# A diffusion trunk step on one core: attention units regrouped so that values, turn and scores of three successive units stand side by side in the weight stream

## The chip, the cores and the metric

The kernel runs on one core of a Trainium2 chip. Its time is device microseconds of one execution; the time before is the median of three runs, 2137.43 us. The engines are named as in the profile: PE is the matrix engine (TensorE), PEld its weight loads, DVE the vector engine, ACT the scalar engine, POOL GpSimd, SP the engine that issues the weight transfers.

## What is computed

Two groups of tokens, 128 context tokens and 256 latent tokens, go through two layers with the same weights (384 token columns in all). A layer is a feed-forward block, a mixing block and a second feed-forward block, each behind a modulated norm. The change is in the mixing block:

```
proj = h @ w_in                                   # 22 blocks of 128 columns, then the gates
a_o = neighbourhood_attention(...)                # NA
b_o = window_attention(rope(q), rope(k), ...)     # SWA, with a sink per head
d_o = softmax(q1 k1) - lam * softmax(q2 k2)       # DF, then @ v, then rmsnorm per head
c_o = hyena(hy_in, lp)                            # long convolution through a DFT
merged = sum_i sigmoid(gate_i) * (branch_i @ w_branch[i])
x = x + g2 * (merged @ w_out)
```

Context tokens attend to context alone; latent tokens also read a cache of 128 keys and values.

## The kernel before

**Tiles.** All weights pass as tiles of 128 output columns through a ring of four buffers: SP loads `raw`, ACT copies it to `hi` (L557, the high part of the split), DVE writes `lo = raw - hi` (L781). For the wider tiles of the gates (1280 columns) DVE makes the first 640 columns of `lo` and POOL the rest (L1197). PE multiplies each of eight 128-row chunks three times (hi by hi, hi by lo, lo by hi), so a tile is 24 matmuls of 384 columns (L1287) into one of four PSUM banks; a gate tile has 6 more for its branch product, into `ps_br`. The split of a tile (the step "feed") is made three tiles before PE needs it.

**The mix.** A layer's mixing block has 22 projection tiles, 32 gate tiles ("fused", four branches of 8, in the order NA, SWA, DF, hyena) and 8 output tiles. Each tile is cut into four parts of 6 matmuls; the fourth part of a gate tile also has the 6 branch matmuls, 12 in all. Between the parts stand the small steps of attention and of the convolution. `mix_plan` writes this order out as one list, and all engines walk that same list, each taking its own share of each step, strictly in order. So the place of a step in the list sets its place in every engine's queue. `paced` spreads a list of steps over a list of parts: a number between two steps is a share of the parts.

**An attention unit.** Each branch has 12 units: block, head half, and token block b = 0, 1, 2. For b = 0 (context) there are 128 keys, else 512 - 128 = 384. A unit has four steps:

- `scores`: PE writes q k into `ps_s` (L1496; the single buffer must be free of the exp before); DVE adds a bias or mask where there is one and takes the negated row maximum (L1062; in SWA also the sink, L1067); ACT takes exp and the row sum into `pr` (L709). DF has two such steps per unit, m = 0 and 1.
- `probs`: DVE alone; it divides by the row sum (L1078, L1088; SWA first L1077), in DF it combines both softmaxes (L1078, L1082 to L1085).
- `turn`: PE transposes `pr` into `ps_t` (L1505, 3 blocks of 128, or 1 for b = 0), ACT copies it to `prT` (L717; the single buffer must be free of the values before).
- `values`: PE multiplies `prT` by the values into `ps_o` (L1522, 6 records in the profile, or 2).

Other small steps that the text speaks of: `short` (DVE alone, a convolution of width 3: L1110 and four times L1114, six per layer, in DF's first half), `gate` (ACT tanh L654, then DVE L986), `rope` (PE L1478, DVE L1044 to L1046, each waiting for the one before), `subnorm`, `subinv`, `subout` (the norm of DF's output), `outs`.

**What orders a feed.** `staged` holds the feed of a tile back until a step of a certain kind comes: `turn` before the change, and at the latest the second part of a projection tile or the fourth of any tile. A `gate` step comes after the first part of the next tile.

Of the kernel before, what the change touches and what calls it, by code (L numbers as in the profile page):

```python
# [35 lines left out]
TB = T // P  # L36
# [22 lines left out]
NA, SWA, DF = range(3)  # L59
# [105 lines left out]
def parts(tiles):  # L165

    return [(*t, part) for t in tiles for part in range(PARTS)]


def paced(tiles, side):  # L170

    out = []
    scale = len(tiles) / sum(x for x in side if not isinstance(x, tuple))
    at, done = 0.0, 0
    for x in side:
        if isinstance(x, tuple):
            out.append(x)
            continue
        at += x * scale
        upto = min(len(tiles), int(at + 0.5))  # L180
        out += tiles[done:upto]
        done = upto
    return out + tiles[done:]


def attention_steps(kind):

    out = []
    if kind == DF:
        out += [("scores", kind, 0, 0), 1.3, ("scores", kind, 0, 1), ("probs", kind, 0), 1.5]
        for u in range(12):
            if u + 1 < 12:
                out.append(("scores", kind, u + 1, 0))
            if u < 6:
                out.append(("short", u))

            if 7 <= u < 7 + TB:  # L200
                out.append(("subinv", 0, u - 7))
            if u == 7 + TB:
                out.append(("subout", 0))
            out += [0.9, ("turn", kind, u), 0.9, ("values", kind, u), 0.1]
            if u + 1 < 12:
                out += [("scores", kind, u + 1, 1), ("probs", kind, u + 1)]
            out.append(1.5)
            if u % 6 == 5:
                out += [("square", u // 6), 0.6, ("subnorm", u // 6)]
        return out + [0.8] + [("subinv", 1, b) for b in range(TB)] + [0.6, ("subout", 1), 0.2]  # L210
    out += [("scores", kind, 0, 0), ("probs", kind, 0), 1.5]
    for u in range(12):
        if u + 1 < 12:
            out.append(("scores", kind, u + 1, 0))
        out += [1.0, ("turn", kind, u)]
        if u + 1 < 12:
            out.append(("probs", kind, u + 1))
        out += [1.2, ("values", kind, u), 0.2]
        if u % 6 == 5:
            out.append(("outs", kind, u // 6))  # L220
    return out


def staged(plan):

    out, fed, gates = [], [], []

    def flush(what):
        out.extend(what)
        what.clear()

    for s in plan:
        tile = s[0] in ("proj", "fused", "out")
        if tile and s[-1] == PARTS - 1:
            flush(fed)
        out.append(s)
        if tile and s[-1] == 0:  # L240
            fed.append(("feed", *s))
            flush(gates)
        if s[0] == "turn" or s[0] in ("proj", "out") and s[-1] == 1:
            flush(fed)
        if s[0] == "fused" and s[-1] == PARTS - 1:
            gates.append(("gate", *s[1:]))
            if s[1:3] == (3, C - 1):
                flush(gates)
    return out


def mix_plan():

    fil = [1.5, ("sinmlp", 1), 5.5]
    for o in range(2):
        for tk in range(TB):
            fil += [("taps", o, tk), 3.3, ("tapsum", o, tk), 0.3]
        fil += [("scale", o), 3.0]
        for fc in range(TB):
            fil += [("filter", o, fc), 0.8]  # L260
    proj = [("proj", k) for k in range(N_PROJ)]

    plan = [("sinmlp", 0)] + [s for pair in zip(parts(proj[0:1]), parts(proj[1:2])) for s in pair]
    plan += paced(parts(proj[2:FILTER_TILES]), fil)
    na = attention_steps(NA)

    cut = na.index(("values", NA, NA_EARLY))
    turns = [("vk", 2), ("vk", 3), ("vk", 4)] + [("rope", j) for j in range(7)]
    rest = []
    for s in na[cut:]:  # L270
        rest.append(s)
        if turns and isinstance(s, tuple) and s[0] == "values":
            rest += [0.5, turns.pop(0), 0.3]
    for s in turns:
        rest += [s, 0.8]
    plan += paced(parts(proj[FILTER_TILES:16]), [("vk", 0), 0.8, ("vk", 1), 0.2] + na[:cut]) + paced(parts(proj[16:]), rest)
    gates = [[("fused", i, n) for n in range(C)] for i in range(4)]
    swa, df = attention_steps(SWA), attention_steps(DF)

    gate_parts = parts(gates[0] + gates[1] + gates[2])  # L280
    until = len(parts(gates[0] + gates[1])) + 1
    plan += paced(gate_parts[:until], swa + df)
    hy = [0.4]
    for o in range(2):
        hy += [("ytok", o, 0), 1.2, ("ytok", o, 1), 1.5]
        for fc in range(TB):
            hy += [("spectrum", o, fc), 0.8]
        hy += [1.0, ("conv", o, 0), 0.8, ("conv", o, 1), 2.0]
    hy += [("hyout", 0), ("hyout", 1), 0.5]
    plan += paced(gate_parts[until:], hy)  # L290
    plan += parts(gates[3])
    out = [parts([("out", c)]) for c in range(C)]
    plan += [("merged", c) for c in range(C)]
    for c in range(C):
        plan += out[c]
        if c:
            plan.append(("xsquare", c - 1))
    return staged(plan)


def build(nc, w_main, w_fused, w_ada, c_rep, consts, vecs, lam, x_in, rope, bias, logdecay, kctx, vctx, mlp_w, mlp_w3, zt, dft,
          y_out, nk, nv):
    ctx = ExitStack()
    with ctx:
# [1464 lines left out]
```

## Time and profile before

| what | value |
|---|---|
| median of three runs | 2137.43 us (2134.98 to 2137.88) |
| the profiled execution's own time | 2135.39 us |
| its span | 2133.6 us |
| PE busy | 2026.4 us, 95% of the span |
| granted clock, mean | 0.98 |

The span is the time between the first and the last instruction of the profiled execution; some 1.8 us of its time lie around it. A share of busy time is a mean over all stages; for what a stage is limited by, its own rows are to be read. The two layers repeat each other: what stands at time t in layer 0 stands at t + 1041.1 us in layer 1.

### The profile page before, as it was taken

The numbers are of one execution on the slowest core, as the hardware profiler recorded it, in microseconds if no ns is written. First come the engines' busy times: TensorE is split into PE (matmuls) and PEld (weight loads), VectorE is DVE, ScalarE is ACT, GpSimd is POOL, SyncE is SP. The second block draws the span as 40 slices with busy tenths as digits, with TensorE's granted clock in tenths as the row PEclk, the third lists the DMA queues.
The fourth block names the chain that finished last, engine by engine and source line by source line (L and its number), as shares of the span: only waits on it lengthen the run. The fifth ranks groups of instructions, "written<-read, shape, count | busy, mean of one in ns | idle before, by whom it ended". The sixth has DMA issues, their size and how long they took to land.

```text
span 2133.6 us, 29756 instructions
## 1 busy us (share of the span) xinstructions
PE 2026.4 (95%) x11052; PEld 1895.2 (89%) x11052; DVE 1446.9 (68%) x2274; ACT 730.6 (34%) x1127; POOL 515.0 (24%) x376
## 2 busy tenths in 40 slices
PE   6999998998899999999999999899899999999998
PEld 6999997877668989999989999888676799899998
DVE  7889897556574458888878778865657544584444
ACT  3322234233343244222342222433333423432222
POOL 2402023111124523120241111320122353320112
PEclk9999998999999999999999999899999999999999
DMA  7776663222122335656556556422211223454332
GB/s 305 255 229 227 224 213 117 83 89 70 54 73 76 102 128 177 206 188 209 195 199 201 193 185 210 149 97 92 79 62 62 75 81 108 138 179 137 128 126 81
DMA packets 82537, 309.53 MB, mean 145 GB/s; under 512 B 9428, under 2 KB 10890, under 8 KB 81536
## 3 DMA queue, kind: packets, MB, share of 16 engines
q1 hardware_dynamic: 80064, 299.36, 42.0%
q0 software_dynamic: 2368, 8.80, 1.2%
q8 instruction: 62, 1.02, 0.2%
q14 instruction: 43, 0.35, 0.1%
HBM read 305.24 MB, written 2.88 MB: 144 GB/s over the span
## 4 chain that ended last, share of the span: by engine, by line
PE 78%; DVE 14%; ACT 4%; issue 2%; DMA 0%; POOL 0%; SPq 0%; DVEq 0%; ACTq 0%; POOLq 0%
PE bank L1287 67%; DVE lo L781 3%; PE ps_br L1287 2%; PE ps_s L1496 2%; PE ps_o L1522 2%; DVE tiny L1062 1%; ACT hi L557 1%; ACT pr L709 1%; DVE areaG L1114 1%; DVE areaM L907 1%; DVE tiny L1077 1%; DVE x L916 1%; ACT areaM L595 1%; DVE areaO L839 1%; ACT prT L717 1%
## 5 line engine op out<-in xcount | busy, mean ns | idle before, releaser
L1287 PE MATMUL bank<-h_hi,hi 128*128 128x384 f32 x2400 | 842.2, 351 | 23.6 <-POOL h_lo L1189 19.2
L1287 PE MATMUL bank<-h_hi,lo 128*128 128x384 f32 x2400 | 812.2, 338 | 0.0
L1287 PE MATMUL bank<-h_lo,hi 128*128 128x384 f32 x2400 | 812.0, 338 | 0.0
L781 DVE TENSOR_TENSOR lo<-raw,hi 128x1024 fp32r<-128x1024 f32 (+1 forms) x396 | 489.4, 1238 | 208.8 <-ACT hi L557 207.3
L557 ACT ACTIVATE hi<-raw 128x1024 fp32r<-128x1024 f32 (+1 forms) x396 | 431.7, 1092 | 523.5 <-PE bank L1287 520.1
L1287 PEld LDWEIGHTS bank<-h_hi,hi 128*128 128x128 f32 x2400 | 457.6, 191 | 79.2 <-issue 51.5
L1287 PEld LDWEIGHTS bank<-h_lo,hi 128*128 128x128 f32 x2400 | 457.9, 191 | 1.4
L1287 PEld LDWEIGHTS bank<-h_hi,lo 128*128 128x128 f32 x2400 | 457.1, 190 | 0.0
L1166 POOL TENSOR_TENSOR g_lo<-areaF,g_hi 128x384 f32 x88 | 161.7, 1838 | 784.6 <-DVE g_hi L894 784.6
L1287 PE MATMUL bank<-g_hi,hi 128*128 128x384 f32 x704 | 237.0, 337 | 2.6 <-POOL g_lo L1166 2.6
L1287 PE MATMUL bank<-g_lo,hi 128*128 128x384 f32 x704 | 236.6, 336 | 0.0
L1287 PE MATMUL bank<-g_hi,lo 128*128 128x384 f32 x704 | 236.6, 336 | 0.0
L907 DVE SCALAR_TENSOR_TENSOR areaM<-areaM,areaO 128x1024 f32<-128x1024 f32 x128 | 206.9, 1616 | 0.0
L1197 POOL TENSOR_TENSOR lo<-raw,hi 128x640 fp32r<-128x640 f32 x64 | 124.1, 1939 | 251.5 <-ACT hi L557 251.5
L907 DVE SCALAR_TENSOR_TENSOR areaO<-areaM,areaO 128x1024 f32<-128x1024 f32 x128 | 169.8, 1326 | 0.0
L916 DVE SCALAR_TENSOR_TENSOR x<-bank,coef,x 128x128 f32<-128x128 f32 x224 | 82.9, 411 | 92.1 <-PE bank L1287 92.0
L614 ACT ACTIVATE areaF<-bank 128x384 f32<-128x384 f32 x88 | 43.3, 492 | 284.8 <-PE bank L1287 284.8
L1287 PEld LDWEIGHTS bank<-g_hi,hi 128*128 128x128 f32 x704 | 132.3, 188 | 3.9 <-POOL g_lo L1166 3.9
L1287 PEld LDWEIGHTS bank<-g_hi,lo 128*128 128x128 f32 x704 | 132.3, 188 | 0.0
L1287 PEld LDWEIGHTS bank<-g_lo,hi 128*128 128x128 f32 x704 | 132.3, 188 | 0.0
L709 ACT ACTIVATE pr<-ps_s,tiny 128x384 f32<-128x384 f32 (+1 forms) x96 | 48.5, 505 | 166.3 <-DVE tiny L1062 166.1
L892 DVE TENSOR_TENSOR areaF<-areaF,bank 128x384 f32<-128x384 f32 x88 | 48.5, 551 | 79.2 <-PE bank L1287 68.7
(209 smaller groups left out, 1754.0 us busy)
## 6 DMA issues: line engine op xcount, KB each, us to landing
raw<-w_main SPq DMA_DIRECT2D x332, 512.0 KB, 4.2
areaM<-w_ada SPq DMA_DIRECT2D x134, 512.0 KB, 3.7
raw<-w_fused SPq DMA_DIRECT2D x64, 640.0 KB, 3.8
areaG<-w_ada SPq DMA_DIRECT2D x7, 512.0 KB, 11.8
areaO<-c_rep SPq DMA_DIRECT2D x3, 1024.0 KB, 5.6
areaE<-bias POOLq DMA_DIRECT2D x2, 1024.0 KB, 7.3
x<-x_in SPq DMA_DIRECT2D x1, 1536.0 KB, 8.4
areaE<-w_ada SPq DMA_DIRECT2D x3, 512.0 KB, 15.4
```

The source lines that it names most:

```text
L557: act.activation(hi[:, slot, 0:width(base)], raw[:, slot, 0:width(base)], ACT.Copy).then_inc(hi_ready, 1)
L614: act.activation(sil[:, s, :], bank[(n0 + j) % RING][:, 0:T], ACT.Silu).then_inc(silu_done, 1)
L709: act.activation(dst, ps_s[:, 0:nk_], ACT.Exp, bias=nm, accum_out=tiny[:, 12 + r % 4:13 + r % 4]).then_inc(exp_done, 1)
L781: dve.tensor_tensor(lo[:, slot, 0:w], raw[:, slot, 0:w], hi[:, slot, 0:w].bitcast(F32), ALU.subtract).then_inc(lo_ready, 1)
L892: dve.tensor_tensor(gf[:, j // 2 % 2, :], sil[:, j // 2 % 2, :], b, ALU.mult).then_inc(gf_ready, 1)
L907: last = dve.scalar_tensor_tensor(out, ada_raw[slot], 1.0, cond_rows[:, g, :], ALU.mult, ALU.mult, accum_out=mod[:, a, g:g + 1])
L916: last = dve.scalar_tensor_tensor(xs, bank[n % RING][:, t0:t1], coef[:, 2, c, g:g + 1], xs, ALU.mult, ALU.add)
L1166: pool.tensor_tensor(g_lo[:, at, :].rearrange("p a t -> p (a t)"), gf[:, s, :], g_hi[:, at, :].rearrange("p a t -> p (a t)").bitcast(F32), ...
L1197: pool.tensor_tensor(lo[:, slot, POOL_FROM:1280], raw[:, slot, POOL_FROM:1280], hi[:, slot, POOL_FROM:1280].bitcast(F32), ALU.subtract).th ...
L1287: last = pe.matmul(dst, wt[:, slot, w], ac[:, c, :], start=c == 0 and k == 0, stop=c == chunks - 1 and k == 2)
L1496: pe.matmul(ps_s[:, 0:k1 - k0], q[a:e, blk, P * b:P * (b + 1)], kt[a:e, kb, k0:k1], start=True, stop=True).then_inc(scores_ready, 1)
L1522: last = pe.matmul(ps_o[64 * hh:64 * hh + 64, P * b:P * (b + 1)], vt[:, ch, col:col + 64], prT[:, P * i:P * (i + 1)], start=i == 0, stop=i ...
```

## The change

The list of attention steps is written anew. Before, a unit's turn, its values, and the scores of the next unit but one stood at up to three places between parts. Now a group `values(u-2), turn(u-1), scores(u)` stands at one place, then a share of parts, `probs(u)`, a share of parts, and the next group; in DF the second score product stands alone one share later, with `short`, `subinv` or `subout` behind it. SWA and DF are one sequence. Feeds are released by `probs`, not by `turn`. In the filter and convolution steps some pairs are put together (`filter` 0 and 1, `spectrum` 0 and 1, `conv` 0 and 1). Nothing is computed differently.

```
-    if kind == DF:
-        out += [("scores", kind, 0, 0), 1.3, ("scores", kind, 0, 1), ("probs", kind, 0), 1.5]
-        for u in range(12):
-            if u + 1 < 12:
-                out.append(("scores", kind, u + 1, 0))
-            if u < 6:
-                out.append(("short", u))
...
-            out += [0.9, ("turn", kind, u), 0.9, ("values", kind, u), 0.1]
-            if u + 1 < 12:
-                out += [("scores", kind, u + 1, 1), ("probs", kind, u + 1)]
-            out.append(1.5)
...
-    out += [("scores", kind, 0, 0), ("probs", kind, 0), 1.5]
-    for u in range(12):
-        if u + 1 < 12:
-            out.append(("scores", kind, u + 1, 0))
-        out += [1.0, ("turn", kind, u)]
-        if u + 1 < 12:
-            out.append(("probs", kind, u + 1))
-        out += [1.2, ("values", kind, u), 0.2]
+    units = [(kind, u) for kind in kinds for u in range(12)]
     out = []
+    for at in range(len(units) + 2):
+        if at >= 2:
+            kind, u = units[at - 2]
+            out.append(("values", kind, u))
             if u % 6 == 5:
+                out.append(("square", u // 6) if kind == DF else ("outs", kind, u // 6))
+        if 1 <= at <= len(units):
+            out.append(("turn", *units[at - 1]))
...
+        kind, u = units[at]
+        out.append(("scores", kind, u, 0))
+        if kind != DF:
+            out += [1.0, ("probs", kind, u), 1.0]
+            continue
+        out += [1.0, ("scores", kind, u, 1)]
...
+        if u < 6:
+            out.append(("short", u))
...
+        out += [1.0, ("probs", kind, u), 1.0]
...
-        if s[0] == "turn" or s[0] in ("proj", "out") and s[-1] == 1:
+        if s[0] == "probs" or s[0] in ("proj", "out") and s[-1] == 1:
             flush(fed)
...
-    swa, df = attention_steps(SWA), attention_steps(DF)
+    both = attention_steps(SWA, DF)
...
-    plan += paced(gate_parts[:until], swa + df)
+    plan += paced(gate_parts[:until], both)
```

How it moves instructions, first on PE in SWA, layer 0, around the scores of unit 5. `ps_t<-kk,pr` is a turn, `ps_o<-prT,vt` values, `ps_s<-kt,q_swa` scores, `bank` a matmul of the weight stream. Before, from the turn of unit 3 on:

```order
L1505 MATMUL ps_t<-kk,pr 128x128
L1287 MATMUL bank<-h_hi,hi 128x384
L1287 MATMUL bank<-h_lo,hi 128x384
L1287 MATMUL bank<-h_hi,lo 128x384
L1287 MATMUL bank<-h_hi,hi 128x384
L1287 MATMUL bank<-h_lo,hi 128x384
L1287 MATMUL bank<-h_hi,lo 128x384
L1522 MATMUL ps_o<-prT,vt 64x128
L1496 MATMUL ps_s<-kt,q_swa 128x384
```

After the change, values of unit 3, turn of unit 4 and scores of unit 5 (line numbers are 5 lower there):

```order
L1282 MATMUL bank<-h_hi,hi 128x384
L1282 MATMUL bank<-h_lo,hi 128x384
L1282 MATMUL bank<-h_hi,lo 128x384
L1517 MATMUL ps_o<-prT,vt 64x128
L1500 MATMUL ps_t<-kk,pr 128x128 x3
L1491 MATMUL ps_s<-kt,q_swa 128x384
L1282 MATMUL bank<-h_hi,hi 128x384
L1282 MATMUL bank<-h_lo,hi 128x384
L1282 MATMUL bank<-h_hi,lo 128x384
```

The turn of unit 3 stood apart, 6 weight matmuls before the values; now the turn between values and scores is that of the next unit, and it comes 12 weight matmuls after its own scores, where there were 24 before.

Then on DVE in DF, layer 0. Before, from `short` 3 through the lo split, the maximum of the second scores of unit 4 and its combination:

```order
L1110 TENSOR_SCALAR areaG<-areaG,vv 128x384
L1114 SCALAR_TENSOR_TENSOR areaG<-areaG,vv 128x127
L1114 SCALAR_TENSOR_TENSOR areaG<-areaG,vv 128x255
L1114 SCALAR_TENSOR_TENSOR areaG<-areaG,vv 128x127
L1114 SCALAR_TENSOR_TENSOR areaG<-areaG,vv 128x255
L781 TENSOR_TENSOR lo<-raw,hi 128x640
L1062 TENSOR_REDUCE tiny<-ps_s 128x1
L1078 RECIPROCAL tiny<-tiny 128x1
L1082 RECIPROCAL tiny<-tiny 128x1
L1083 TENSOR_TENSOR tiny<-tiny 128x1
L1084 TENSOR_SCALAR pr<-pr,tiny 128x384
L1085 SCALAR_TENSOR_TENSOR pr<-pr,tiny 128x384
```

After the change, from the same maximum of unit 4 on (L1057 is the maximum, L1105 and L1109 are `short` 4, L1073 to L1080 the combination, L776 the lo split):

```order
L1057 TENSOR_REDUCE tiny<-ps_s 128x1
L1105 TENSOR_SCALAR areaG<-areaG,vv 128x384
L1109 SCALAR_TENSOR_TENSOR areaG<-areaG,vv 128x127
L1109 SCALAR_TENSOR_TENSOR areaG<-areaG,vv 128x255
L1109 SCALAR_TENSOR_TENSOR areaG<-areaG,vv 128x127
L1109 SCALAR_TENSOR_TENSOR areaG<-areaG,vv 128x255
L1073 RECIPROCAL tiny<-tiny 128x1
L1077 RECIPROCAL tiny<-tiny 128x1
L1078 TENSOR_TENSOR tiny<-tiny 128x1
L1079 TENSOR_SCALAR pr<-pr,tiny 128x384
L1080 SCALAR_TENSOR_TENSOR pr<-pr,tiny 128x384
L776 TENSOR_TENSOR lo<-raw,hi 128x640
```

The `short` stood before the second maximum, and the lo split too; now the `short` stands between the second maximum and the combination, and the lo split behind the combination.

## Rows read from the trace of the kernel before

**Rows 1.** the page: busy time by engine, share of the span, instructions

```profile
PE 2026.4 (95%) x11052; PEld 1895.2 (89%) x11052; DVE 1446.9 (68%) x2274; ACT 730.6 (34%) x1127; POOL 515.0 (24%) x376
```

**Rows 2.** windows: length, busy PE PEld DVE ACT POOL, granted clock, DMA share, GB/s

```profile
418.60:491.00 72.40, 67.91 (x362) 54.26 (x360) 41.48 (x82) 25.04 (x56) 9.77 (x9) 1.00 0.27 87
491.00:557.00 66.00, 59.59 (x310) 46.19 (x311) 36.35 (x87) 23.36 (x62) 13.18 (x6) 1.00 0.20 70
557.00:649.00 92.00, 83.72 (x399) 63.12 (x399) 62.21 (x140) 37.85 (x86) 23.61 (x16) 0.96 0.19 65
649.00:661.00 12.00, 10.28 (x59) 9.50 (x59) 6.96 (x8) 7.09 (x10) 4.10 (x3) 1.00 0.17 56
568.88:575.71 6.83, 6.34 (x17) 4.76 (x17) 4.06 (x12) 1.12 (x4) 0.00 (x0) 0.50 0.24 89
```

**Rows 3.** waits of PE between 418.6 and 661 us: total, times, longest

```profile
PE ps_o L1522 <- ACT prT L717: 9.7, 16, 0.9
PE ps_s L1496 <- ACT pr L709: 3.2, 6, 1.7
PE ps_t L1505 <- DVE pr L1088: 2.2, 4, 0.9
```

**Rows 4.** timeline of PE: how the stream is left and entered again

```profile
563.13 0.34 PE L1287 MATMUL bank<-h_hi,lo 128*128 128x384 f32 x1
563.30 0.27 PE L1505 MATMUL ps_t<-kk,pr 128*128 128x128 f32 x1
...
563.59 0.33 PE L1287 MATMUL bank<-h_lo,hi 128*128 128x384 f32 x1
...
564.29 0.34 PE L1287 MATMUL bank<-h_hi,lo 128*128 128x384 f32 x1
564.56 0.43 PE L1522 MATMUL ps_o<-prT,vt 128*64 128x128 f32 x2
564.93 0.91 PE L1496 MATMUL ps_s<-kt,areaG 32*128 32x384 f32 x2
...
566.05 0.34 PE L1287 MATMUL bank<-h_lo,hi 128*128 128x384 f32 x1
```

**Rows 5.** timeline of PE: four transposes ahead of a score product

```profile
418.14 0.49 PE L1467 MATMUL ps_t<-kk,areaG 128*128 128x128 f32 x3
...
418.67 0.48 PE L1496 MATMUL ps_s<-kt,areaG 64*128 64x128 f32 x2
```

**Rows 6.** timeline of DVE: one DF unit, then one short convolution

```profile
576.16 0.55 DVE L986 SCALAR_TENSOR_TENSOR areaM<-areaG,ps_br 128x384 f32<-128x384 f32 x1 [2.79 <-ACT areaG L654]
578.80 0.56 DVE L1062 TENSOR_REDUCE tiny<-ps_s 128x1 f32<-128x384 f32 x1 [2.08 <-PE ps_s L1496]
580.10 0.16 DVE L1078 RECIPROCAL tiny<-tiny 128x1 f32<-128x1 f32 x1 [0.74 <-ACT pr L709]
...
580.49 0.16 DVE L1083 TENSOR_TENSOR tiny<-tiny 128x1 f32<-128x1 f32 x1
...
581.14 0.62 DVE L1085 SCALAR_TENSOR_TENSOR pr<-pr,tiny 128x384 f32<-128x384 f32 x1
...
582.38 1.77 DVE L1114 SCALAR_TENSOR_TENSOR areaG<-areaG,vv 128x127 f32<-128x127 f32 x4
```

**Rows 7.** timeline of ACT: tanh of a gate, hi split of a wide tile

```profile
575.64 0.48 ACT L654 ACTIVATE areaG<-bank 128x384 f32<-128x384 f32 x1
...
582.79 1.26 ACT L557 ACTIVATE hi<-raw 128x1280 fp32r<-128x1280 f32 x1
```

**Rows 8.** timeline, DVE and POOL: a small operation while POOL makes lo

```profile
509.08 2.19 POOL L1197 TENSOR_TENSOR lo<-raw,hi 128x640 fp32r<-128x640 f32 x1 [7.63 <-ACT hi L557]
...
509.78 1.51 DVE L1077 TENSOR_TENSOR tiny<-tiny 128x1 f32<-128x1 f32 x1
```

**Rows 9.** timeline of DVE: an NA unit whose scaling stands behind the lo split

```profile
441.21 1.23 DVE L781 TENSOR_TENSOR lo<-raw,hi 128x1024 fp32r<-128x1024 f32 x1 [1.69 <-ACT hi L557]
...
442.54 0.42 DVE L1088 TENSOR_SCALAR pr<-pr,tiny 128x384 f32<-128x384 f32 x1
```

More of the change, by code:

```diff
@@ L183, in paced, with attention_steps @@
     return out + tiles[done:]
[L186 removed]
+def attention_steps(*kinds):
+    units = [(kind, u) for kind in kinds for u in range(12)]
     out = []
[L192 to L220 removed]
@@ new lines, in attention_steps @@
+    for at in range(len(units) + 2):
+        if at >= 2:
+            kind, u = units[at - 2]
+            out.append(("values", kind, u))
+            if u % 6 == 5:
+                out.append(("square", u // 6) if kind == DF else ("outs", kind, u // 6))
+        if 1 <= at <= len(units):
+            out.append(("turn", *units[at - 1]))
+        if at == len(units):
+            out.append(2.0)
+            continue
+        if at > len(units):
+            break
+        kind, u = units[at]
+        out.append(("scores", kind, u, 0))
+        if kind != DF:
+            out += [1.0, ("probs", kind, u), 1.0]
+            continue
+        out += [1.0, ("scores", kind, u, 1)]
+        if u == 7:
+            out.append(("subnorm", 0))
+        if u < 6:
+            out.append(("short", u))
+        if 8 <= u < 8 + TB:
+            out.append(("subinv", 0, u - 8))
+        if u == 8 + TB:
+            out.append(("subout", 0))
+        out += [1.0, ("probs", kind, u), 1.0]
@@ L221, in attention_steps @@
+    if DF in kinds:
+        out += [0.6, ("subnorm", 1), 0.8] + [("subinv", 1, b) for b in range(TB)] + [0.6, ("subout", 1), 0.2]
     return out
@@ L256, in mix_plan @@
         for tk in range(TB):
[L257 to L260, printed above, removed]
+            fil += [("taps", o, tk), 3.5, ("tapsum", o, tk)]
+        fil += [0.3, ("scale", o), 3.0, ("filter", o, 0), ("filter", o, 1), 1.6, ("filter", o, 2), 0.8]
     proj = [("proj", k) for k in range(N_PROJ)]
@@ L271, in mix_plan @@
         rest.append(s)
-        if turns and isinstance(s, tuple) and s[0] == "values":
-            rest += [0.5, turns.pop(0), 0.3]
+        if turns and isinstance(s, tuple) and (s[0], turns[0][0]) in (("probs", "vk"), ("scores", "rope")):
+            rest += [0.5, turns.pop(0)] if s[0] == "probs" else [turns.pop(0)]
     for s in turns:
@@ L277, in mix_plan @@
     gates = [[("fused", i, n) for n in range(C)] for i in range(4)]
-    swa, df = attention_steps(SWA), attention_steps(DF)
+    both = attention_steps(SWA, DF)
     gate_parts = parts(gates[0] + gates[1] + gates[2])
     until = len(parts(gates[0] + gates[1])) + 1
-    plan += paced(gate_parts[:until], swa + df)
+    plan += paced(gate_parts[:until], both)
     hy = [0.4]
     for o in range(2):
[L285 to L288, printed above, removed]
+        hy += [("ytok", o, 0), 1.2, ("ytok", o, 1), 1.5, ("spectrum", o, 0), ("spectrum", o, 1), 1.6, ("spectrum", o, 2), 1.8,
+               ("conv", o, 0), ("conv", o, 1), 2.8]
     hy += [("hyout", 0), ("hyout", 1), 0.5]
```

## The prediction

> **What bounds the kernel now.** The page comes first: PE is busy 95% of the span [rows 1], so the time is PE's work plus PE's idle time, and other engines matter only where PE waits for them. The windows come next, since that 95% is a mean. The reader is to see that PE's idle time per layer lies in the attention steps: 72.40 - 67.91 = 4.5 us in NA, 6.4 in SWA, 8.3 in DF and 1.7 behind DF, 20.9 us in all [rows 2]. DVE is busy 62.2 of 92 us in DF and no engine but PE is near full there, so these are waits for a chain of steps through engines that work in order, not for a full engine. In one stretch of 6.83 us in DF the granted clock is 0.50, the lower of TensorE's two levels, 1.2 GHz, just after PE had stood 1.75 us for an exp; it costs 3.4 us per layer [rows 2]. The waits view then says for what: of the 20.9 us, 9.7 are values that wait for ACT's copy of the transposed probabilities, 3.2 scores that wait for an exp, 2.2 turns that wait for DVE's scaling in NA and SWA [rows 3]. Last comes PE's timeline, for what it costs to leave the weight stream.
>
> **Fewer interruptions: about nothing.** Between scores of NA's first and values of DF's last unit the list leaves the weight stream 90 times per layer before and 57 after. What is one worth? Steady weight matmuls start 0.175 us apart (563.59 to 564.29 is four). A turn of one block alone: from the weight matmul at 563.13 to the next but one at 563.59 are 0.46 us, 0.35 would be two steps, so it costs 0.11, just what one transpose costs inside a row of them ((0.49 - 0.27) / 2) [rows 4, 5]. A turn alone is interrupted for nothing. Values and scores together leave at 564.29 and are back at 566.05: entry 0.27 where a step is 0.175, first weight matmul back 0.29 [rows 4], so some 0.2 us for entry and exit, with 0.1 more between values and scores. Now the turn goes between these two. Its neighbours there are not in the trace of before; the nearest is four transposes ahead of scores, 0.53 us for four [rows 5], 0.09 more than four times 0.11, and I take this, and the same in front of it. Before, 19 units had values and scores side by side (by the list) and the turn alone for nothing; these lose some 0.1 us each, the rest win 0.1 to 0.2. With each neighbour priced so over the whole list I get 194.3 us of PE work before and 194.5 after. If the turn cost nothing between them, 34 units would save 2 x 0.1 to 0.2 us, 7 to 9 us per layer; that is the other end. In the filter and convolution steps seven interruptions go, between operations that fill all rows of the array as the weights do: 0 to 1.4 us, I take 0.7.
>
> **What goes: the waits of the values.** Before, the copy of a turn had about one part (6 matmuls, 1.05 us) before the values needed it. Now it has two parts and a score product, over 3 us. The 9.7 us go [rows 3]. The tiny DVE operation L1077 (SWA) also took 1.51 us behind a lo split that POOL shared [rows 8]; with the feed behind `probs` it comes clear of POOL.
>
> **What comes: the turn is now close behind its own scores.** From the end of scores to the turn there are 12 weight matmuls (2.25 us) and the values of the unit before (0.8 us for 6 records; 2 take 0.37 up to the next operation [rows 4]): a slack of 3.0 us, 2.55 where those values are of a b = 0 unit, and 1.05 us more if a part with branch matmuls (or a third part) lies between. Before it was 24 matmuls and the scores of the next unit. PE stands in order, so a late turn holds values, scores and stream behind it. The chain that the turn needs, branch by branch:
>
> NA. DVE's scaling is done 2.4 us after the end of the scores (bias 0.43, maximum 0.56, exp 0.77 with its sum, reciprocal and scaling 0.6), which fits. But at four units the feed falls between the scores and `probs` (a projection tile releases it at its second part): ACT's hi split, then DVE's 1.23 us, stand before the scaling. From the end of the maximum (441.21 - 1.69 = 439.52) to the end of the scaling at 442.96 that took 3.4 us [rows 9], so 4.55 from the scores on. Against slacks of 3.2 to 3.6: waits of 0.3, 0.95, 0.95, 1.1, 3.4 with the odd tenth. The last ropes keep some 2.1, since each still waits for DVE's three operations of the one before. NA after: 5.5 (before 4.5 up to 491 us and the rest just behind it, 4.9).
>
> SWA. The chain is 2.9 us and fits, but in five units a gate now lies between the scores and `probs`: tanh 0.48 behind the exp on ACT, then 0.55 on DVE [rows 6, 7], so 4.0. Waits: 1.0, 1.45, 0, 1.0, 1.45. SWA after: 4.9 (before 6.0).
>
> DF, units 0 to 5. From the end of the second scores: maximum 0.6, reciprocal 0.74 after it, combination to 581.76, 2.96 after the maximum's start [rows 6], so 3.05: would just fit. But `short` now stands between: 0.5 and 1.77 us [rows 6], less the 0.7 of exp that it covers, so 4.6, and 5.15 with a gate; b = 0 units some 0.65 less. Slacks by the list: 3.0, 2.55, 4.05, 4.05, 2.55, 4.05. Waits 1.0, 2.6, 0.6, 0, 2.0, 1.1: 7.3 us. That is the lower end, without POOL. For ACT goes on to the hi split right after the exp: it ends 2.6 us after the scores (1.3 + 1.26 [rows 7]), and POOL then works 1.5 to 2.2 us on its part of lo, just when the combination starts at 3.0 to 3.3. L1077 has two inputs in SBUF and took 1.51 us beside POOL [rows 8]; its twin L1083, 0.16 alone [rows 6], and L1085 would be held likewise, to 4.2 or 4.7. Then the waits are 1.7, 3.4, 0.6, 0.6, 2.9, 1.9: 11.1 us. The Trainium skill says the same of the mechanism (GPSIMD Engine Reference, "Key points": POOL shares its SBUF interfaces with VectorE, in contention where that has two SBUF inputs or a two-port mode). By that rule the 11.1 stand; the trace agrees with it at L1077 [rows 8], and at L1083 it can't say, which is 0.16 in this unit without POOL [rows 6].
>
> DF, the rest. Second scores wait for the first exp: 1.45 against 1.18 us of one part, in five units, 1.4 us, up to 3 where the lo split is late. Units 6 to 11 have no `short`, but a gate and `subinv` in one of them: 2.2 us, with POOL up to 6.3. DF after: 7.3 + 1.4 + 2.2 = 10.9, up to 20.4 (before 8.3).
>
> Behind DF: `subnorm` stands right behind the last values and waits for two ACT operations, 1.2 us; in exchange the branch product waits less: 1.5 (before 1.7).
>
> **The sum per layer.** 5.5 + 4.9 + 10.9 + 1.5 = 22.8 us, up to 32.3, against 20.9: a loss of 1.9 to 11.4 us. I take 8, nearer to the upper end, since L1077 is the nearest row and most of DF's first units have a feed. Less 0.7 for the filter and convolution steps: 7.3 us per layer, 14.6 in both. On the profiled execution's own time: 2135.4 + 14.6 = 2150. The three runs have their median 2 us above that execution; 2150 is meant for either. Two runs of this kernel can be told apart from about 0.2% on, 4.3 us.
>
> **The rivals.**
> 1. The transposes ride for nothing between values and scores: -8 us per layer against +7.3, so 2134: no change. For it: the turn alone costs nothing today. Against it: the scores use 32 or 64 rows, and every change between these and full-height operations shows its 0.1 us [rows 4, 5].
> 2. The lower end of the waits (POOL holds nobody): +1.2 per layer, 2138: no change. If the stretch at the lower clock goes too, since the 1.75 us wait for an exp that stood before it is gone, 3.4 per layer come back: 2131, a shade faster.
> 3. Faster: the values' waits go and the turns do not wait, because DVE comes to `short`, gate and combination earlier than I reckon. Place: the turn in DF. It decides once the chain of 4.6 us falls under the slack of about 3.4. Price: -9.7 and half of the other DF waits, and the stretch at half clock: some -13 per layer, 2109. Against it: `short` is on the same engine as the combination and ahead of it.
> 4. Slower still: single waits of 2 to 3 us in DF bring the lower clock more often. Each such stretch, if as long as the one seen, costs 3.4 us [rows 2]: two more per layer give 2164.
>
> **How the numbers follow.** The forecast 0.46, rival 4 0.14, rivals 1 and 2 0.18 together, of which 0.04 are faster by over 0.2%, rival 3 0.22. Slower by over 0.2%: 0.60; the same 0.14; faster 0.26. The forecast alone spans 2140 to 2157 (2135.4 and twice 11.4 - 0.7). The range has to reach into rival 3 and rival 4: 2115 to 2168.
>
> **What the profile after would show.** Values waiting for L712 (the copy): none. Turns in DF waiting for L1080 with 7 to 11 us per layer, those in NA and SWA for L1083 with 3 to 8. L1072 at 0.16 us throughout. L1078 in DF at over 0.5 us where POOL works. PE's work in the attention steps without waits unchanged within 2 us per layer. The forecast is wrong if turns in DF wait less than 4 us per layer, or if turn to scores starts 0.05 us apart and not 0.2.

## The result and the profile after

The changed kernel takes 2185.78 us, the median of four runs (2183.90 to 2188.74), where the kernel before took 2136.90 on the same chip. The ratio is 1.0231, 95% interval 1.0213 to 1.0249: it is 49 us slower. The forecast was 2150 with a range of 2115 to 2168: the sign was right, the size was not.

The page of the kernel after, engine by engine (busy time, share of the span, instructions), answers to [rows 1]:

```profile
PE 2058.7 (94%) x11052; PEld 1921.9 (88%) x11052; DVE 1440.3 (66%) x2274; ACT 736.6 (34%) x1127; POOL 510.5 (23%) x376
```

PE has the same 11052 instructions, and is busy 32.3 us longer. So the loss is not only waiting: the matmuls themselves took longer. The windows of the same stages, which answer to [rows 2] (length, busy PE PEld DVE ACT POOL, granted clock, DMA share, GB/s; NA, SWA, DF, and the piece behind it):

```profile
417.10:491.30 74.20, 69.19 (x362) 56.31 (x362) 39.60 (x83) 26.01 (x56) 10.36 (x9) 0.98 0.28 88
491.30:552.00 60.70, 56.88 (x294) 44.54 (x294) 29.21 (x85) 23.69 (x60) 13.24 (x6) 0.99 0.21 72
552.00:673.30 121.30, 102.24 (x420) 77.43 (x418) 68.81 (x141) 38.99 (x86) 20.72 (x16) 0.85 0.15 49
673.30:686.00 12.70, 9.92 (x58) 8.98 (x57) 6.87 (x8) 7.74 (x10) 4.52 (x3) 1.00 0.18 53
```

Length less PE busy is 5.0, 3.8, 19.1 and 2.8 us of idle time, 30.7 a layer where it was 20.9. DF grew from 8.3 to 19.1 and the piece behind it from 1.7 to 2.8; NA and SWA together idle 8.8 where they idled 10.9. And DF has a mean granted clock of 0.85. The stretches at the lower clock, by windows laid on them (the same columns):

```profile
560.31:563.72 3.41, 3.41 (x12) 2.97 (x11) 0.13 (x1) 0.67 (x2) 0.00 (x0) 0.50 0.55 192
570.55:580.80 10.25, 10.25 (x27) 7.61 (x26) 5.01 (x14) 2.32 (x6) 0.00 (x0) 0.50 0.19 64
601.27:604.70 3.43, 3.43 (x12) 3.37 (x11) 0.47 (x1) 0.67 (x2) 0.00 (x0) 0.50 0.55 191
621.75:632.00 10.25, 10.25 (x24) 7.05 (x24) 2.84 (x8) 4.65 (x8) 0.00 (x0) 0.50 0.21 66
659.31:669.55 10.24, 10.24 (x27) 7.65 (x27) 3.65 (x9) 2.59 (x7) 0.00 (x0) 0.50 0.20 66
488.62:492.04 3.42, 3.42 (x11) 3.11 (x11) 1.64 (x4) 0.00 (x0) 0.00 (x0) 0.50 0.57 169
```

The first five lie in DF, the last behind the last rope. They add up to 41.0 us at 1.2 GHz in a layer's attention steps, where before there were 6.8 [rows 2]. PE is busy in each from end to end: what runs there runs at half speed, so half of such a stretch is lost. The waits of PE in the same 269 us (total, times, longest), against [rows 3]:

```profile
PE ps_t L1500 <- DVE pr L1080: 18.7, 9, 3.5
PE ps_t L1500 <- DVE pr L1083: 6.5, 8, 1.1
PE ps_br L1473 <- DVE areaG L1041: 2.0, 1, 2.0
PE ps_br L1282 <- DVE o_lo L1099: 1.8, 1, 1.8
PE ps_t L1524 <- ACT areaE L724: 1.0, 1, 1.0
PE ps_s L1491 <- ACT pr L704: 0.4, 2, 0.2
PE ps_s L1491 <- DVE kt L1041: 0.3, 1, 0.3
```

The waits of the values are gone, and the turns wait for DVE: 18.7 us for the combination in DF (L1080), 6.5 for the scaling in NA and SWA (L1083). How a fall of the clock comes about, on PE's timeline at DF's unit 1 (start, us, instruction, idle time before it and its releaser):

```profile
566.70 0.43 PE L1517 MATMUL ps_o<-prT,vt 128*64 128x128 f32 x2
570.12 0.55 PE L1500 MATMUL ps_t<-kk,pr 128*128 128x128 f32 x3 [2.99 <-DVE pr L1080]
570.60 1.64 PE L1491 MATMUL ps_s<-kt,areaG 32*128 32x384 f32 x2
```

The turn comes 2.99 us late, and 0.43 us after it starts, at 570.55, the clock falls for 10.25 us; the two score matmuls behind it take 1.64 us, where they took 0.91 [rows 4]. All six stretches begin like this, 0.3 to 1.7 us after the end of a wait: of 2.12, 2.99, 3.46, 1.78 and 3.38 us in DF, and of 2.04 for the last rope. Not every wait does it: the one of 2.72 us that ends at 612.70 is followed by no fall before 621.75, and the four of 1.09 to 1.11 us (at 465.66, 515.95, 545.33 and 590.17) by none at all. What decides between them is not shown here.

Why the turn is late, on the timelines of DVE and POOL at DF's unit 5 (L1057 the second maximum, L1105 and L1109 `short`, L981 the gate, L1073 to L1080 the combination; on POOL L1250 adds the gated branch to the sum, L1192 makes its part of `lo`):

```profile
605.87 0.56 DVE L1057 TENSOR_REDUCE tiny<-ps_s 128x1 f32<-128x384 f32 x1 [4.13 <-PE ps_s L1491]
606.35 0.47 DVE L1105 TENSOR_SCALAR areaG<-areaG,vv 128x384 f32<-128x384 f32 x1
606.85 1.78 DVE L1109 SCALAR_TENSOR_TENSOR areaG<-areaG,vv 128x127 f32<-128x127 f32 x4
608.67 0.55 DVE L981 SCALAR_TENSOR_TENSOR areaG<-areaG,ps_br 128x384 f32<-128x384 f32 x1
...
609.52 0.79 DVE L1078 TENSOR_TENSOR tiny<-tiny 128x1 f32<-128x1 f32 x1
610.35 1.65 DVE L1079 TENSOR_SCALAR pr<-pr,tiny 128x384 f32<-128x384 f32 x1
612.03 0.62 DVE L1080 SCALAR_TENSOR_TENSOR pr<-pr,tiny 128x384 f32<-128x384 f32 x1
```

```profile
609.30 1.00 POOL L1250 TENSOR_TENSOR areaM<-areaM,areaG 128x384 f32<-128x384 f32 x1 [11.57 <-DVE areaG L981]
610.25 1.53 POOL L1192 TENSOR_TENSOR lo<-raw,hi 128x640 fp32r<-128x640 f32 x1
```

From 605.87 to 612.65 are 6.8 us. Four things make 5.2 of them: the short convolution (2.3), the gate (0.5), and two operations each held to about the end of one of POOL: L1078, 0.16 alone, ends at 610.31 with POOL's addition; L1079, 0.42 alone, ends at 612.00, after POOL's split, which ends at 611.78. The rest is the maximum, two reciprocals and L1080.

Last, what a group costs where nothing is late, on PE's timeline in SWA:

```profile
524.33 0.34 PE L1282 MATMUL bank<-h_hi,lo 128*128 128x384 f32 x1
524.60 0.87 PE L1517 MATMUL ps_o<-prT,vt 128*64 128x128 f32 x6
525.40 0.33 PE L1500 MATMUL ps_t<-kk,pr 128*128 128x128 f32 x1
525.66 0.91 PE L1491 MATMUL ps_s<-kt,q_swa 64*128 64x384 f32 x2
526.50 0.45 PE L1282 MATMUL bank<-h_hi,hi 128*128 128x384 f32 x1
```

The transpose and the scores start 0.26 us apart here. In both layers together 68 score products stand right behind a turn: 45 start 0.20 us after its last transpose, nearly all of them behind a turn of three, and 23 start 0.26 us after it, nearly all behind a turn of one. None comes near the 0.05 us that the prediction named as the sign against it.

### The profile page after: what moved, and what is told of

Same layout as the page of the kernel before. It is cut to its first block, busy times and chain, and to the rows that moved or that the text cites. A ratio compares the mean times of both kernels' runs of the same rounds, so it can differ in the third digit from the quotient of the medians.

```text
span 2186.9 us, 29760 instructions
## 1 busy us (share of the span) xinstructions
PE 2058.7 (94%) x11052; PEld 1921.9 (88%) x11052; DVE 1440.3 (66%) x2274; ACT 736.6 (34%) x1127; POOL 510.5 (23%) x376
## 4 chain that ended last, share of the span: by engine, by line
PE 81%; DVE 13%; ACT 3%; issue 2%; DMA 0%; POOL 0%; SPq 0%; DVEq 0%; ACTq 0%; POOLq 0%
PE bank L1282 67%; PE ps_s L1491 3%; PE ps_br L1282 3%; DVE lo L776 2%; PE ps_t L1500 1%; PE ps_o L1517 1%; DVE areaG L1109 1%; DVE tiny L1057 1%; DVE areaM L902 1%; ACT hi L552 1%; DVE pr L1080 1%; DVE pr L1079 1%; DVE x L911 1%; ACT areaM L590 1%; DVE areaO L834 1%
## 5 line engine op out<-in xcount | busy, mean ns | idle before, releaser
L776 DVE TENSOR_TENSOR lo<-raw,hi 128x1024 fp32r<-128x1024 f32 (+1 forms) x396 | 479.7, 1213 | 168.3 <-ACT hi L552 167.1
L1282 PEld LDWEIGHTS bank<-h_lo,hi 128*128 128x128 f32 x2400 | 462.6, 193 | 2.1 <-issue 0.6
L1192 POOL TENSOR_TENSOR lo<-raw,hi 128x640 fp32r<-128x640 f32 x64 | 119.7, 1870 | 243.5 <-ACT hi L552 243.2
L1057 DVE TENSOR_REDUCE tiny<-ps_s 128x1 f32<-128x384 f32 (+1 forms) x96 | 45.0, 469 | 94.8 <-PE ps_s L1491 93.4
## 6 DMA issues: line engine op xcount, KB each, us to landing
areaE<-w_ada SPq DMA_DIRECT2D x3, 512.0 KB, 15.4
```

What stands on the lines that cost most here:

```text
L776: dve.tensor_tensor(lo[:, slot, 0:w], raw[:, slot, 0:w], hi[:, slot, 0:w].bitcast(F32), ALU.subtract).then_inc(lo_ready, 1)
L1057: red = dve.tensor_reduce(nm, ps_s[:, 0:k1 - k0], AX_X, ALU.max, negate=True)
L1192: pool.tensor_tensor(lo[:, slot, POOL_FROM:1280], raw[:, slot, POOL_FROM:1280], hi[:, slot, POOL_FROM:1280].bitcast(F32), ALU.subtract).th ...
L1282: last = pe.matmul(dst, wt[:, slot, w], ac[:, c, :], start=c == 0 and k == 0, stop=c == chunks - 1 and k == 2)
```

## The experiments

**One sum for all kernels.** For each kernel I took the stretch from the first scores of layer 0 to the first branch product behind `subout`, PE's idle time in it and its time at 1.2 GHz. If time at 1.2 GHz counts half, length less idle less half of the 1.2 GHz time must be one number. Before: 241.3 - 20.9 - 3.4 = 217.0. After: 267.5 - 30.7 - 20.5 = 216.3.

| kernel | median us | ratio (interval) | length | idle | at 1.2 GHz | rest |
|---|---|---|---|---|---|---|
| before | 2136.90 | 1 | 241.3 | 20.9 | 6.8 | 217.0 |
| after | 2185.78 | 1.0231 (1.0213 to 1.0249) | 267.5 | 30.7 | 41.0 | 216.3 |
| DF as before | 2119.91 | 0.9924 (0.9905 to 0.9944) | 233.1 | 14.6 | 3.4 | 216.8 |
| NA, SWA as before | 2192.00 | 1.0262 (1.0242 to 1.0282) | 270.6 | 33.7 | 41.0 | 216.4 |
| short first | 2167.51 | 1.0153 (1.0133 to 1.0174) | 254.8 | 22.9 | 30.7 | 216.6 |
| fill | 2160.27 | 1.0114 (1.0095 to 1.0134) | 253.3 | 15.4 | 6.8 | 234.5 |
| half fill | 2170.74 | 1.0154 (1.0140 to 1.0168) | 257.7 | 22.9 | 17.1 | 226.3 |
| gates behind probs | 2150.05 | 1.0069 (1.0051 to 1.0087) | 247.5 | 18.7 | 23.9 | 216.9 |
| pairs undone | 2185.39 | 1.0238 (1.0221 to 1.0255) | 266.3 | 31.0 | 37.5 | 216.6 |
| POOL's split short | 2154.14 | 1.0090 (1.0076 to 1.0104) | 251.0 | 22.1 | 23.9 | 217.0 |
| three moves | 2118.84 | 0.9921 (0.9905 to 0.9938) | 231.2 | 10.4 | 6.8 | 217.4 |
| DF as before, feeds | 2114.09 | 0.9891 (0.9876 to 0.9907) | 230.2 | 11.9 | 3.4 | 216.6 |
| DF as before, gates | 2121.49 | 0.9927 (0.9913 to 0.9940) | 233.1 | 13.3 | 6.8 | 216.4 |
| DF as before, both | 2121.16 | 0.9932 (0.9916 to 0.9949) | 235.3 | 12.7 | 13.7 | 215.8 |

The rest is 215.8 to 217.4 us in all but the two filled ones, which have added work: PE's work at full clock did not change, however the steps are grouped. Everything that happened in this stretch is idle time and clock. (Short first, gates behind probs, POOL's split short and three moves have one more piece of 3.4 us at 1.2 GHz in layer 0, which begins just behind the stretch and is not in the table. Idle and 1.2 GHz time are of the profiled execution; the ratios are to runs of the kernel before on the same chip.)

**DF as before.** NA and SWA in the new order, DF in the old, its feeds released by `turn` as then.

```
-    both = attention_steps(SWA, DF)
+    swa, df = attention_steps(SWA), old_steps(DF)
...
-    plan += paced(gate_parts[:until], both)
+    plan += paced(gate_parts[:25], swa) + paced(gate_parts[25:until], df)
```

> The changed kernel with DF in the order of before (its feeds released by the turn again), NA and SWA in the new order. In the trace after, a layer is 24.6 us longer: 9.8 us are more PE idle time in the attention steps, and PE has 41.0 us at the lower clock there where it had 6.8. Theory A (DF's late turns make the waits, the waits make the lower clock): nearly all of the loss goes with DF's order, since NA and SWA of the trace after have 8.9 us of idle time against 10.9 before; expected 2132 to 2142 us. Rival B (the merged groups themselves are dear on PE, wherever they stand): 24 of 36 units keep them, so two thirds of the loss stay, 2165 to 2175 us.

2119.91 us, below both: the whole loss sits in DF's order (with the release of its feeds), and the rest of the change is a gain of 16 us, which theory A had not expected. Its waits of PE:

```profile
PE ps_t L1538 <- DVE pr L1121: 5.8, 8, 1.1
PE ps_s L1529 <- ACT pr L742: 3.2, 8, 0.7
...
PE ps_o L1555 <- ACT prT L750: 1.2, 2, 0.7
```

But for the last rope no wait in NA, SWA or DF is over 1.1 us here, and there is one stretch at the lower clock, of 3.4 us, behind that rope.

**NA and SWA as before**, DF new: the other half. SWA has 26 parts of the stream here.

```
-    na = attention_steps(NA)
+    na = old_steps(NA)
...
+    swa, df = old_steps(SWA), attention_steps(DF)
```

> The other half: NA and SWA in the order of before, DF in the new order. Theory A: the whole loss stays, 2178 to 2190 us, with 28 to 36 us per layer at the lower clock in DF. Rival B: one third of the loss, 2150 to 2155 us.

2192.00, 2 us over the upper end of what was expected. It has the same 41.0 us at 1.2 GHz as the kernel after and 3.0 us more idle time. Of the 41.0 us, 37.6 lie in DF in both kernels, more than the 28 to 36 that were expected; the other 3.4 lie here in SWA, behind a turn that waits 1.56 us. So DF's new order brings nearly all of the lower clock without the other two.

**Short first.** In DF, `short`, `subinv` and `subout` ahead of the second scores.

```
-        out += [1.0, ("scores", kind, u, 1)]
         if u < 6:
             out.append(("short", u))
...
+        out += [1.0, ("scores", kind, u, 1)]
```

> The changed kernel with short, subinv and subout behind the first scores of a DF unit, no longer between the second maximum and the combination. Theory A: the turns of DF's units 0 to 5, which wait 12.4 us per layer in the trace after, wait some 4 us, the one of unit 10 2 and not 3.4; the single waits get under 2 us and the lower clock falls from 41 to under 20 us per layer. 8 to 10 us of waits and up to 10 us of clock per layer: 2145 to 2160 us. Rival C (not short but POOL's hold on DVE makes the turns late): the turns still wait over 8 us per layer, 2170 us or more.

2167.51: 18 us back, less than theory A expected and more than rival C allowed. DF's turns wait 10.8 us in place of 18.7, over the 8 us of rival C, so `short` is one cause and not the only one. The idle time fell by 7.8 us, the time at 1.2 GHz only by 10.3, for waits of up to 3.1 us are left.

**Fill.** Ahead of seven late turns in each DF, PE makes transposes that nothing reads, behind the wait for a free `ps_t` and ahead of the wait for `probs`; DVE's chain is the same, but PE works while it waits. Nothing is left out.

```
+FILL = {0: 16, 1: 24, 3: 8, 4: 28, 5: 22, 6: 14, 10: 28}
...
+                        for _ in range(FILL.get(u, 0) if ty == DF else 0):
+                            pe.transpose(ps_t[:, 384:512], ident, ident)
```

> The changed kernel with idle transposes of the identity (columns 384 to 512 of ps_t, read by nobody) ahead of the turns of DF units 0, 1, 3, 4, 5, 6 and 10: 16, 24, 8, 28, 22, 14 and 28 of them at 0.11 us, a little less than these turns wait. The waits end no sooner, PE is only busy in them, 15 us per layer. Theory A (idle PE is what lowers the clock): the lower clock in the attention steps falls from 41 to under 15 us per layer and 10 to 15 us per layer come back, 2156 to 2168 us. Rival D (the lower clock has another cause than these waits, such as the kind of work): the clock stays as it is and the time is 2184 us or more.

2160.27: work was added, no chain was shortened, and 25.5 us came back. DF's window in this kernel, against 0.85 above:

```profile
553.00:661.00 108.00, 104.08 (x575) 81.79 (x575) 68.95 (x141) 39.34 (x87) 20.84 (x16) 1.00 0.17 56
```

So the fall of the clock follows from PE standing idle in these waits, and it, not the waits themselves, is the larger part of the loss. The 6.8 us that are left are two pieces outside DF: one behind the last rope, and one in SWA, 1.7 us after the end of a wait of 1.11 us.

**Half fill.** Half as many transposes at the same places (8, 12, 4, 14, 11, 7, 14).

> The changed kernel with half the extra transposes of the filled one ahead of the same differential turns (8, 12, 4, 14, 11, 7 and 14 in place of 16, 24, 8, 28, 22, 14 and 28), so that about 7.7 us of the 15.4 us of waits that the full set covered stay idle. It leaves out nothing and adds work that nothing reads. If the time at 1.2 GHz depends on how much TensorE stands idle there, it ends between the 41.0 us a layer of the changed kernel and the 6.8 of the filled one: at 20 to 30 us a layer the time is 2168 to 2178. If it is all or nothing: 2160 (all gone) or 2186 (none gone).

2170.74, with 17.1 us at 1.2 GHz, below the 20 to 30 that were named, between the others: not all or nothing. DF's longest wait is now 1.8 us.

**Gates behind probs.** The gate of a tile of the first two branches (these tiles pass during SWA and DF) is held back until the next `probs`, so it no longer stands between a unit's scores and its combination.

```
             fed.append(("feed", *s))
-            flush(gates)
+            if s[0] != "fused" or s[1] > 1:
+                flush(gates)
+        if s[0] == "probs" or tile and s[-1] == 2:
+            flush(gates)
```

> The changed kernel with one rule altered: the gate step of a tile of the first two branches comes behind the next probs (at the latest behind the third part of the next tile), not behind the first part. So no gate, and no addition of POOL that follows a gate, lies between a unit's scores and its probs. Theory A (gate and POOL between the last maximum and the combination make the turns of SWA 2, 4, 8, 10 and of DF 1, 4, 5, 6, 10 late): the four waits in SWA of 0.67 to 1.11 us go, the turns in DF wait some 12 us and not 21.5 (DF in all), the clock follows: 2145 to 2165 us. Rival C (gates are hidden beside the exp and short alone counts): 2175 us or more.

2150.05. DF's turns wait 9.5 us in place of 18.7, and 17 of the 41 us at 1.2 GHz are gone:

```profile
PE ps_t L1503 <- DVE pr L1083: 9.5, 7, 3.0
PE ps_t L1503 <- DVE pr L1086: 3.3, 5, 1.1
```

The gates do more here than the short convolutions. A gate brings POOL's addition with it; how much is the gate's own time and how much the addition's was not taken apart. One of the stretches that are left stands behind a short wait. It lasts 6.83 us, and the last wait ahead of it is a turn's of 1.06 us that ends at 641.72, 2.0 us before (the columns are those of the windows above):

```profile
643.70:650.53 6.83, 6.83 (x19) 5.32 (x18) 2.55 (x7) 1.76 (x6) 1.53 (x2) 0.50 0.30 98
```

**POOL's split short.** From the fifth gate tile on, POOL's part of `lo` is 32 columns in place of 640 (`POOL_TO` is 1280 for the first four wide tiles, then 672). The other 608 keep older values, so the low part of the gate weights is left out there.

```
-                pool.tensor_tensor(lo[:, slot, POOL_FROM:1280], ...
+                pool.tensor_tensor(lo[:, slot, POOL_FROM:POOL_TO], ...
```

> The changed kernel with GpSimd's part of the lo split of a gate tile cut from 640 to 32 columns from the fifth gate tile on, so that this operation no longer takes 1.53 us; the other 608 columns keep older values, so the low part of the gate weights is left out there. Order, semaphores and all work of the other engines stay. In the changed kernel the combination or the short convolution stood beside this operation in most late differential units, and single operations of the vector engine took 0.69 (for 0.16), 1.65 (for 0.42), and four of 1.78 together took 3.06 to 3.15. Theory A, those long durations come from GpSimd's operation: the vector engine's operations go back to their short durations there, the differential turns' waits fall from 18.7 us a layer to 9 to 12 (GpSimd's 1.0 us addition behind a gate still holds the scaling behind it), the time at 1.2 GHz falls from 41 us a layer to between 10 and 28, 2145 to 2165. Theory B, the vector engine is slow there for another reason (reads of the same rows, its own queue): waits within 1.5 us of 18.7, 2182 to 2188.

2154.14. Nothing changed on DVE's own list, and its long operations are short again; unit 5 (all line numbers 1 or 2 higher):

```profile
605.37 0.16 DVE L1074 RECIPROCAL tiny<-tiny 128x1 f32<-128x1 f32 x1
...
605.76 0.78 DVE L1079 TENSOR_TENSOR tiny<-tiny 128x1 f32<-128x1 f32 x1
606.58 0.42 DVE L1080 TENSOR_SCALAR pr<-pr,tiny 128x384 f32<-128x384 f32 x1
```

```profile
605.53 1.00 POOL L1252 TENSOR_TENSOR areaM<-areaM,areaG 128x384 f32<-128x384 f32 x1 [13.10 <-DVE areaG L982]
606.48 0.25 POOL L1194 TENSOR_TENSOR lo<-raw,hi 128x32 fp32r<-128x32 f32 x1
```

The scaling is back from 1.65 to 0.42 beside the short split; the tiny operation in front of it is still 0.78, held by the addition that was left as it was. DF's turns wait 9.6 us: with POOL's split gone from DF, 9.1 of the 18.7 go, 17.1 us at 1.2 GHz, and 30 to 32 us of the kernel. The gains of short first, of the gates and of this kernel (18, 36 and 32 us) are not to be added up, for they shorten the same chains.

**Pairs undone.** The pairs of `filter`, `spectrum` and `conv` taken apart again in the changed kernel.

```
-        fil += [0.3, ("scale", o), 3.0, ("filter", o, 0), ("filter", o, 1), 1.6, ("filter", o, 2), 0.8]
...
+        fil += [("scale", o), 3.0]
+        for fc in range(TB):
+            fil += [("filter", o, fc), 0.8]
...
```

> The changed kernel with the filter, spectrum and conv steps as before, each interrupting the stream by itself. The prediction priced the pairs at a gain of 0.7 us per layer, so this should be 1 to 2 us slower than the changed kernel, 2184 to 2190 us. The rival, that the pairs bring new waits outside the attention steps, would show as 3 us or more faster, under 2182 us.

2185.39 against 2185.78 for the kernel after: their intervals overlap, the pairs are worth nothing that shows.

**Three moves.** Short first, gates behind probs, and the feeds of the projection tiles behind `probs` too, no longer at a tile's second part. The lines of the third move:

```
-        if s[0] == "probs" or s[0] in ("proj", "out") and s[-1] == 1:
+        if s[0] == "probs" or s[0] == "proj" and s[1] < FILTER_TILES and s[-1] == 1 or s[0] == "out" and s[-1] == 1:
```

> The changed kernel with three moves: short, subinv and subout behind the first scores, gates behind probs, and in NA the feed behind probs alone (not at the second part of a projection tile). All three take work of DVE or ACT from between a unit's last scores and its turn. Theory A: PE idle time in the attention steps falls from 30.7 to 10 to 15 us per layer and the lower clock from 41 to under 10 us; 2105 to 2130 us, so faster than before. Rival E (two parts are too short a distance for DF's chain even when nothing is in it, since POOL's lo still holds DVE): idle over 18 us, 2140 us or more.

2118.84: the grouping itself is not what costs. With the same groups of values, turn and scores, and other vector work out of the unit's chain, the kernel is 67 us faster than after and 17 faster than before.

**DF as before, with both, and with each of the moves.** The feeds' move and the gates' move (for SWA only), on top of DF as before.

> The first experiment (NA and SWA in the new order, DF in the order of before, 2119.9 us) with the gates of SWA behind probs and NA's feeds behind probs. Its idle time has 3.0 us of turns behind a feed in NA and 2.8 us behind a gate in SWA per layer. Theory A: these go, 4 to 6 us per layer, 2108 to 2113 us. If the gates and feeds only move the wait to another step, 2117 us or more.

> The differential units keep the order of before, the other two kinds have the new one (the kernel of 2119.91 us), and one thing is moved: the vector work that a projection tile feeds during the neighbourhood units is let out only behind the next "probs", no longer behind a tile's second part. The kernel with this and with the sliding-window gates moved had no gain (2121.16), although the waits of its turns fell from 6.0 to 2.0 us a layer; its values waits rose from 1.2 to 3.6 and its time at 1.2 GHz from 3.4 to 13.7 us. Theory A, the two moves are separate and the loss sits in the differential units, where the gates' last piece came one piece earlier: this kernel alone gains what it takes off the neighbourhood turns (2.97 us a layer down to about 0.3), 2.5 us a layer, 2113 to 2116. Theory B, the feeds' move itself pushes vector work into the differential units or the tail: 2119 to 2123.

> The same kernel of 2119.91 us with the other move alone: the gates of the sliding-window units stand behind "probs" in place of in front of the turns; the pieces of the stream are shared out as there (25 pieces to these units, where the kernel with both moves had 26). Theory A: the sliding-window turns' waits (2.8 us a layer) go to about 0.6 and nothing changes in the differential units: 2115 to 2118. Theory B, what took the gain away comes with the gates (a gate now lies before the first differential unit's work): values waits over 3 us and more than 10 us at 1.2 GHz a layer, 2121 to 2126.

Both together give 2121.16, no gain, where theory A expected 2108 to 2113. The feeds alone give 2114.09, as their theory A said, and the fastest kernel here, 1.09% below before:

```profile
PE ps_s L1529 <- ACT pr L742: 3.2, 8, 0.7
PE ps_t L1538 <- DVE pr L1121: 3.1, 5, 1.1
```

The gates alone give nothing: 2121.49, though the turns wait 1.5 us less; a second stretch of 3.4 us at 1.2 GHz came in. That time lies in theory B's range, but its sign doesn't show: the values wait 1.2 us. Values waits over 3 us came only with both moves (3.6 us, and 13.7 us at 1.2 GHz). There DF's scores also wait 1.75 us for an exp at 562.29, with 6.83 us at 1.2 GHz beside it, as in the kernel before. Both together also give SWA one part more of the stream (26, not 25), so DF's units stand elsewhere; whether the shift or the two moves together made those waits wasn't tried, and stays open.

## Why the prediction was wrong

**Right.** The page and windows were read rightly: the new cost is PE waiting for a chain, in DF. The values waits went, the turns took their place. The idle time was forecast as 22.8 to 32.3 us a layer, with +8 taken; it is 30.7, which is +9.8. It stays inside the 32.3 by its sum, not by each of its parts: DF's turns wait 18.7 us, where the prediction's own signs had 7 to 11. By branch, NA is 5.0 us (5.5 forecast), SWA 3.8 (4.9), DF 19.1 (10.9 up to 20.4), behind DF 2.8 (1.5). Unit by unit the first six DF turns wait 2.12, 2.99, 0, 1.09, 3.46 and 2.72 us; the working had 1.7, 3.4, 0.6, 0.6, 2.9 and 1.9 with POOL. Together 12.4 against 11.1; units 6 to 11 wait 6.3, which was their upper end, and the second scores' waits for an exp are 0.4 in place of 1.4 to 3.

Fewer interruptions are worth nothing that shows: the rest of the sum is 216.3 against 217.0, and turn to scores starts 0.20 us apart, so rival 1 is out. L1077, now L1072, is 0.16 us in all 24 units. L1083, now L1078, is 0.69 and 0.79 beside POOL. Rival 2, that POOL holds nobody, is refuted by the kernel with the short split.

**The failed step.** It is the clock: the central sum put the change in the time at half clock at nothing, and rival 4 took two more stretches per layer at a cost of 3.4 us each, with a chance of 0.14. Measured are 34.2 us a layer more at 1.2 GHz, worth 17.1, where rival 4 had 6.8. With idle time this makes 9.8 + 17.1 - 0.7 of PE work = 26.2 us a layer, 52.4 in two layers; the profiled spans differ by 53.3. Without the clock the measured idle time would have given 2135.4 + 2 x (9.8 - 0.7) = 2154, inside the range. The mechanism stood among the rivals. Its price for one stretch came from the one in the trace of before, 6.83 us at half speed, and holds in the mean: the six last 3.4 to 10.25 us, 6.83 on average, which nothing in the working made sure of. What failed is their number: none more in the central sum, two more in rival 4, five more in the trace. That there would be so many was not worked out, though the trace of before has a wait of 1.75 us with a fall right at its end, at 568.88:

```profile
568.85 0.95 PE L1496 MATMUL ps_s<-kt,areaG 32*128 32x384 f32 x1 [1.75 <-ACT pr L709]
```

The forecast itself had four waits of 1.7 to 3.4 us in DF's first half alone. The filled kernel shows it: with PE kept busy, 41.0 becomes 6.8 and the same order costs 25.5 us less.

**Also missed.** The forecast alone begins at 2135.4 + 2 x 1.2 = 2138 by its own terms, not at 2140. POOL's addition behind each gate (L1250, 1.0 us) was not in the working; it holds L1078 just as the split holds L1079. So units 6 and 10 wait 1.78 and 3.38 us with no `short` in them; in unit 6 the two hold-ups are 0.63 and 1.24 us, as long as the whole wait. And POOL holds the short convolution itself where the two meet: at 585.66 and 594.95 its four operations take 3.15 and 3.06 us, not 1.78. The wait of the last rope, 2.04 us where it was 1.72, shows the same: L1041 takes 1.77 us there for 0.43, from 486.45 to 488.22, over POOL's split from 486.41 to 487.94. The gain outside DF's own order was put at about nothing, and is 8.2 us a layer in the kernel with DF as before: 6.3 of idle time and 1.7 of clock. Of the 6.3, 2.9 are in NA and SWA (8.0 where it was 10.9), and 3.4 in DF (4.9 where it was 8.3), whose units have the old order there but stand beside other parts of the stream. The largest piece in DF is one wait of scores for an exp, 1.75 us before and at most 0.74 there, and the stretch at 1.2 GHz behind it is gone. What makes that wait shorter was not taken apart.

The Trainium skill (TensorE: Matmul & The Clock Gate, Terms) has the cost of a stretch at the lower clock as its time times one minus the granted share, half of it at 4/8. The table's last column agrees, within 1.6 us in 217. By that rule the 34.2 us more at 1.2 GHz cost 17.1 a layer; how many stretches there would be no row of before gave.

## What to carry to other kernels

When steps are moved closer together, count what stands on every in-order engine between producer and consumer, the operations of POOL that hold a DVE operation up included, and price a single wait of two or three microseconds on PE not by itself alone but with the stretch at half clock that may follow: here the second was worth more than the first. A wait of about 1 us can stand ahead of such a stretch too. If a wait can't be removed, work of no use in it may be cheaper than idling (2160 against 2186 us), but taking other vector work out of the chain is better (2119). Undo a change by stage before judging it: this one held a gain of 16 us beside a loss of 66 in one stage.

## What the runs showed of the hardware

- Some vector operations that meet one of POOL's are held to about that one's end, however small they are: L1078 from 0.16 to 0.79 us beside the addition, L1079 from 0.42 to 1.65 beside the split, the four L1109 from 1.78 to 3.15. The Trainium skill (GPSIMD Engine Reference, "1. Specifications") names contention for DVE operations with two SBUF inputs or in a two-port mode. The rows agree for L1078 and L1109, which have two inputs. L1079 has one tensor input and a column of scalars, and is held too. Its times fit the second case: 256 elements more cost it 0.13 us (0.29 to 0.42), and cost L1080, with two inputs, 0.27 (0.35 to 0.62), so it runs at twice the rate. That it does so by a second port is not shown by a row. The maxima and the gate, which read PSUM, and the reciprocals of one column were not lengthened where they met POOL (0.56, 0.56 and 0.16 us). The times at 128 elements, for a unit with b = 0:

```profile
589.44 0.29 DVE L1079 TENSOR_SCALAR pr<-pr,tiny 128x128 f32<-128x128 f32 x1
589.76 0.35 DVE L1080 SCALAR_TENSOR_TENSOR pr<-pr,tiny 128x128 f32<-128x128 f32 x1
```

- In the attention steps of the kernel after PE ran at 1.2 GHz for stretches of 3.4 to 10.2 us, each beginning within 1.7 us after a wait of 1.8 to 3.5 us, while it was busy all through them. With transposes in seven of these waits 6.8 us were left of 41.0, with half as many 17.1.
- The length of one wait does not decide it. A stretch also began behind shorter last waits: 1.06 us (gates behind probs, 643.70), 1.11 (fill, 548.28), 1.16 (DF as before with both moves, 616.87), 1.05 (with the gates alone, 531.11) and 0.77 (three moves, 563.77), each 0.9 to 2.1 us after the end of the wait. Most waits of 0.75 to 1.2 us had none behind them, nor had the one of 2.72 us.
